# Block products by a seven-product scheme in the input products of a diffusion backbone's second block, and another order of the opening

## The reference, cut to what matters

```python
xx = h_shift - h
xr, xw, xk, xv, xa, xg = (h + xx * mu[m] for m in range(6))
r = xr @ w_r; k = xk @ w_k; v = xv @ w_v; zg = xg @ w_z     # 1024 x 2048 each
w_lo = tanh(xw @ w1); a_lo = xa @ a1                        # 1024 x (2*64) each
```

## Time and profile before

| | |
|---|---|
| median of 3 runs | 2981.92 us (2981.19 to 2993.5) |
| the profiled execution, own time | 2982.58 us |
| its span in the trace | 2980.7 us |
| mean granted TensorE clock | 0.954 |
| TensorE matmul | 2700.6 us busy, 91% |
| VectorE, ScalarE, GpSimd | 1448.8, 744.6, 266.5 us busy |

### The profile page before, as it was taken

The page is one execution under the profiler, slowest core; times in us unless marked ns, Lnnn a source line. Parts: engine busy times, 40 slices in busy tenths (PEclk is TensorE's granted clock), DMA queues, the critical chain, the costliest instruction groups (busy, mean ns, idle before and its releaser), DMA issues. The chain is left out here.

```text
span 2980.7 us, 73744 instructions
## 1 busy us (share of the span) xinstructions
PE 2700.6 (91%) x33498; PEld 1678.5 (56%) x33498; DVE 1448.8 (49%) x2198; ACT 744.6 (25%) x1311; POOL 266.5 (9%) x420
## 2 busy tenths in 40 slices
PE   5999999989999959999999998688898898888699
PEld 1555555543444534455555554477777777777543
DVE  3222222228999940230101000689989989888201
ACT  3121221212112100220100100445454454443100
POOL 1000000000000000000000000012212112121100
PEclk8999999999999979999999999699999999999699
DMA  4222222251313136333222231111111111110161
GB/s 183 72 90 87 83 90 83 83 175 35 106 45 97 36 123 227 126 98 103 91 93 92 95 101 66 36 30 39 40 36 41 38 35 45 40 29 28 54 238 50
DMA packets 211569, 242.83 MB, mean 81 GB/s; under 512 B 22952, under 2 KB 158456, under 8 KB 210133
## 3 DMA queue, kind: packets, MB, share of 16 engines
q1 hardware_dynamic: 199090, 194.97, 20.4%
q0 software_dynamic: 11552, 43.27, 3.9%
q10 hardware_dynamic: 644, 0.24, 0.0%
HBM read 184.95 MB, written 53.49 MB: 80 GB/s over the span
## 5 line engine op out<-in xcount | busy, mean ns | idle before, releaser
L105 PE MATMUL ps<-hT,hw 128*128 128x512 f32 (+1 forms) x2048 | 562.1, 435 | 5.5 <-ACT hT L119 5.5
L105 PEld LDWEIGHTS ps<-hT,hw 128*128 128x128 f32 x2048 | 313.0, 192 | 251.7 <-issue 251.7
L1751 POOL TENSOR_SCALAR e_Sd<-e_S,e_pcd 128x64 f32<-128x64 f32 x256 | 164.3, 658 | 779.3 <-DVE e_S L108 317.7
L105 PE MATMUL ps<-m_spare 128*128 128x512 f32 (+1 forms) x768 | 209.8, 434 | 0.0
L113 DVE TENSOR_SCALAR hcv<-hpad,hpc 128x641 f32<-128x641 f32 x48 | 29.6, 616 | 301.5 <-ACT hpad L119 301.5
L119 ACT ACT_TABLE_LOAD x87 | 111.6, 1283 | 239.6 <-PE ps L105 233.6
L105 PEld LDWEIGHTS ps<-m_spare 128*128 128x128 f32 x768 | 116.9, 191 | 91.8 <-issue 91.8
L119 ACT ACTIVATE m_w<-ps 128x640 f32<-128x640 f32 x64 | 45.1, 704 | 484.7 <-PE ps L105 484.7
L105 PE MATMUL ps<-f_w,f_y 128*128 128x512 f32 x320 | 140.2, 600 | 9.7 <-DMA f_y<-scratch_y_d 8.9
L116 DVE TENSOR_TENSOR m_w<-ps,m_w 128x640 f32<-128x640 f32 x16 | 13.2, 825 | 258.8 <-ACT m_w L119 258.8
L108 DVE SCALAR_TENSOR_TENSOR m_spare<-m_room,col 128x640 f32<-128x640 f32 (+2 forms) x32 | 21.0, 713 | 237.0 <-PE ps L105 237.0
(11 more groups left out here) (276 smaller groups left out, 4798.3 us busy)
## 6 DMA issues: line engine op xcount, KB each, us to landing
hw<-in_hy_w_in SPq DMA_DIRECT2D x64, 512.0 KB, 3.9
scratch_rkvz_d<-m_w POOLq DMA_DIRECT2D x64, 320.0 KB, 3.4
m_room<-in_ada_w SPq DMA_DIRECT2D x24, 512.0 KB, 6.5
scratch_vx_d<-hot POOLq DMA_DIRECT2D x32, 320.0 KB, 3.1
conv_room<-scratch_vx_d SPq DMA_DIRECT2D x8, 1280.0 KB, 9.1
aw<-in_ada_w SPq DMA_DIRECT2D x8, 1024.0 KB, 18.1
f_w<-in_rw_w_o SPq DMA_DIRECT2D x32, 256.0 KB, 4.1
scratch_g_d<-hg POOLq DMA_DIRECT2D x16, 320.0 KB, 2.5
```

What stands on the lines that cost most here:

```text
L105: return nc.tensor.matmul(out, lhsT, rhs, start=first, stop=last)
L1751: po_.did(nc.gpsimd.tensor_scalar(Sd[:, q, :], S_at[:, n, q, :], pcd[i % 3][:, u:u + 1], None, MUL), ("Sd", i, n))
```

## The change

Three things in `middle`, one in `startup`.

**Products.** The four first blocks of r are left as they are. The other 60 blocks are taken in 30 pairs `PAIRS` (6 of r, 8 each of k, v, z). A pair is a product of a 256 x 1024 by a 1024 x 640 matrix, cut into 2 x 2 blocks: output channels in two halves of 128, input channels in two halves of 512 (four groups, `KH`), tokens in two halves of 320 (`HT`). Seven block products (P1 to P7) take the place of eight, after the Winograd form of Strassen's scheme. Each is four `mm` of 128 x 320, into one bank of a ring of eight. Four sums of weight blocks `S` (128 x 512 each) are made on GpSimd per pair, and four sums of token blocks `T` (128 x 1280 each) on VectorE once per matrix. VectorE puts the results together by seven additions of 128 x 320 per pair; ScalarE copies P1. For z the sigmoid is taken of the finished result in SBUF, and VectorE multiplies in SBUF, in the next pair's turn.

**Weights.** SyncE fetches a pair at a time (1 MB) into one of three slots; two of them lie where the rows `x` and the bias were, so the first two loads wait until the last row tile is normalised.

**Order.** The small products w and a come right behind the first four blocks, and their mixes are made first. The mixes and token sums of the next matrix are spread over the pairs of the present one, two instructions in each (`beside`).

**The opening.** `ORDER` is another one, and the programs of VectorE and ScalarE follow it, as the diff shows.

```diff
-    ORDER = ["cond", "fcols", "F0", "bias", "a0", "cols", "a1", "x0", "x1", "F1", "x2", "a2", "x3", "x4", "a3", "x5", "x6", "a4", "x7", "F2",
-             "a5", "a6", "a7", "shift", "scale"]
+    ORDER = ["cond", "fcols", "bias", "a0", "F0", "x0", "a1", "x1", "a2", "F1", "x2", "a3", "x3", "cols", "a4", "x4", "F2", "a5", "x5", "a6",
+             "x6", "a7", "x7", "shift", "scale"]
+    COLS_AT = 4
...
+                channels(0)
                 sine(0)
-                channels(0)
-                channels(1)
+                for k in range(1, COLS_AT):
+                    channels(k)
                 sine(1)
-                for k in range(2, KD):
+                for k in range(COLS_AT, KD):
                     channels(k)
-                sine(2)
                 a.wait_ge(pe_.sem, pe_.now("a7"))
                 for c, at in enumerate(ROWS):
                     ac_.did(act(mrow[at, :], ps[at, 0:2, :].rearrange("p b n -> p (b n)"), ACT.Copy), ("half row", c))
+                sine(2)
...
+                        pe.wait_ge(ac_.sem, ac_.now(("h", COLS_AT - 1)))
...
+                    if k == COLS_AT:
+                        pe.wait_ge(dv_.sem, dv_.now("cols"))
...
-                argument(0)
-                v.wait_ge(pe_.sem, pe_.now("cols"))
-                dv_.did(nc.vector.tensor_copy(col[:, :, :], ps[:, 4, :].rearrange("p (g n) -> p g n", g=4)), "cols")
...
+                argument(0)
                 argument(1)
+                v.wait_ge(pe_.sem, pe_.now("cols"))
+                dv_.did(nc.vector.tensor_copy(col[:, :, :], ps[:, 4, :].rearrange("p (g n) -> p g n", g=4)), "cols")
...
+    PAIRS = [(b, q) for b in BIG for q in range(KE // 2) if (b, 2 * q) not in UNITS[0:U]]
+    HT = T // 2
+    KH = KD // 2
+    ORDER = ("P1", "P6", "P7", "P5", "P2", "P4", "P3")
+    TAKEN = {"P1": "p1", "P6": "U2", "P7": "U3", "P5": "U4", "P2": "C11", "P4": "C21", "P3": "C12"}
+    RESULTS = [(n, g) for g in range(len(PAIRS)) for n in ORDER]
+    bank = lambda n, g: ps[:, (4 + RESULTS.index((n, g))) % 8, 0:HT]
...
+        sums = [w2_at[:, U * T:U * T + KD * T], o_at[:, :]]
+        mix = [flat(a, KD) for a in mixes]
+        low = {"w": mix[1], "a": flat(sums[1], KD)}
+        TT = [[flat(a[:, n * KH * HT:(n + 1) * KH * HT], KH) for n in range(4)] for a in sums]
...
+        S = [flat(y_at[:, KD * T + 3 * D + n * KH * P:KD * T + 3 * D + (n + 1) * KH * P], KH) for n in range(4)]
+        rw2 = [flat(a, KD) for a in (spare[:, KD * T:KD * T + 2 * D], xb[:, 0:2 * D], xb[:, 2 * D:4 * D])]
...
+                def load_pair(g):
+                    b, q = PAIRS[g]
+                    slot = (g + 1) % SLOTS
+                    if g >= SLOTS:
+                        wait(pe_, "P3", g - SLOTS)
+                    sp.dma_start(rw2[slot], A[f"rw_w_{b}"][0].rearrange("(k p) n -> p k n", p=P)[:, :, 2 * q * P:(2 * q + 2) * P]).then_inc(s_rw2[slot], 16)
...
-                for m in range(U, len(UNITS)):
-                    load_unit(m)
+                wait(dv_, "normed", NT - 1)
+                load_pair(0)
+                load_pair(1)
+                wait(pe_, "proj", *UNITS[2])
+                for g in range(2, len(PAIRS)):
+                    load_pair(g)
...
+                def weight_sum(g, n):
+                    if g == len(PAIRS):
+                        return
+                    slot = (g + 1) % SLOTS
+                    A_ = lambda i, j: rw2[slot][:, j * KH:(j + 1) * KH, i * P:(i + 1) * P]
+                    po.wait_ge(s_rw2[slot], 16 * (g // SLOTS + 1))
+                    if g:
+                        wait(pe_, ("P5", "P6", "P7", "P3")[n], g - 1)
+                    if n in (1, 3):
+                        wait(po_, "S", g, n // 2)
+                    p, q, op = ((A_(1, 0), A_(1, 1), ADD), (S[0], A_(0, 0), SUB), (A_(0, 0), A_(1, 0), SUB), (A_(0, 1), S[1], SUB))[n]
+                    po_.did(nc.gpsimd.tensor_tensor(S[n], p, q, op), ("S", g, n))
+
+                def store(b, u):
+                    m = UNITS.index((b, u))
                     po.dma_start(A["rkvz_d"][BIG.index(b), u * P:(u + 1) * P, :], rout[m % U]).then_inc(s_o[m % U], 16)
+                for b, u in UNITS[0:U]:
+                    wait(ac_, "out", b, u)
+                    store(b, u)
+                wait(dv_, "normed", NT - 1)
+                for n in range(4):
+                    weight_sum(0, n)
+                for g, (b, q) in enumerate(PAIRS):
+                    for n in (2, 0, 1, 3):
+                        weight_sum(g + 1, n)
+                    if b == "z":
+                        wait(dv_, "gated_z", 2 * q + 1)
+                        store(b, 2 * q + 1)
+                        wait(dv_, "gated_z", 2 * q)
+                        store(b, 2 * q)
+                    else:
+                        wait(dv_, "C21", g)
+                        store(b, 2 * q + 1)
+                        wait(dv_, "C12", g)
+                        store(b, 2 * q)
...
-                for n in range(4, len(JOBS)):
-                    b, u = JOBS[n]
-                    steps, *label = TAKEN[n - 4]
-                    wait(steps, *label)
-                    weights(n)
+                        last = product(n, prompt, k)
+                    pe_.did(last, ("proj", *UNITS[n]))
+                pe.wait_ge(s_lw, 64)
+                for n, b in enumerate("wa"):
+                    wait(ac_, "out", *UNITS[n])
                     for k in range(KD):
-                        if u == 0:
-                            wait(dv_, "mix", b, k)
-                        product(n, image, 0, k)
-                        last = product(n, prompt, LS, k)
-                    pe_.did(last, ("proj", b, u))
+                        wait(dv_, "mix", b, k)
+                        lhsT = lw[n][:, k, :, :].rearrange("p z r -> p (z r)")
+                        mm(pair[n][:, image], lhsT, low[b][:, k, image], k == 0, k == KD - 1)
+                        last = mm(pair[n][:, prompt], lhsT, low[b][:, k, prompt], k == 0, k == KD - 1)
+                    pe_.did(last, ("lora", b))
+
+                for g, (b, q) in enumerate(PAIRS):
+                    slot = (g + 1) % SLOTS
+                    A_ = lambda i, j: rw2[slot][:, j * KH:(j + 1) * KH, i * P:(i + 1) * P]
+                    at = BIG.index(b) % 2
+                    B_ = lambda j, c: mix[at][:, j * KH:(j + 1) * KH, c * HT:(c + 1) * HT]
+                    T_ = TT[at]
+                    OPERANDS = {"P1": (A_(0, 0), B_(0, 0)), "P2": (A_(0, 1), B_(1, 0)), "P3": (S[3], B_(1, 1)), "P4": (A_(1, 1), T_[3]),
+                                "P5": (S[0], T_[0]), "P6": (S[1], T_[1]), "P7": (S[2], T_[2])}
+                    if g == 0:
+                        wait(ac_, "out", *UNITS[U - 1])
+                        wait(ac_, "lora", "a")
+                    pe.wait_ge(s_rw2[slot], 16 * (g // SLOTS + 1))
+                    if b != "r":
+                        wait(dv_, "mix", b, KD - 1)
+                    wait(dv_, "T", b, 3)
+                    for n in ORDER:
+                        at_ring = RESULTS.index((n, g))
+                        if at_ring >= 8:
+                            before, its = RESULTS[at_ring - 8]
+                            wait(ac_ if before == "P1" else dv_, TAKEN[before], its)
+                        if n in ("P5", "P6", "P7", "P3"):
+                            wait(po_, "S", g, ("P5", "P6", "P7", "P3").index(n))
+                        lhsT, rhs = OPERANDS[n]
+                        for k in range(KH):
+                            last = mm(bank(n, g), lhsT[:, k, :], rhs[:, k, :], k == 0, k == KH - 1)
+                        pe_.did(last, (n, g))
...
+                mixed("w", low["w"], range(KD))
+                mixed("a", low["a"], range(KD))
+                wait(dv_, "mix_prompt")
+                for n in range(4):
+                    token_sum("r", n)
...
+                    if share < 4:
+                        mixed(to, mix[at], (2 * share, 2 * share + 1))
+                    else:
+                        token_sum(to, 2 * share - 8)
+                        token_sum(to, 2 * share - 7)
...
+                for g, (b, q) in enumerate(PAIRS):
+                    m = UNITS.index((b, 2 * q))
+                    even, odd = rout[m % U], rout[(m + 1) % U]
+                    wait(ac_, "p1", g)
+                    wait(pe_, "P6", g)
+                    dv_.did(tt(u2, bank("P6", g), p1, ADD), ("U2", g))
+                    wait(pe_, "P7", g)
+                    wait(dv_, "U2", g)
+                    dv_.did(tt(u3, bank("P7", g), u2, ADD), ("U3", g))
+                    v.wait_ge(s_o[(m + 1) % U], 16 * (m // U))
                     v.wait_ge(s_o[m % U], 16 * (m // U))
-                    dv_.did(tt(rout[m % U], pair[n % 4][:, 0:T], sig, MUL), ("out", "z", u))
+                    wait(pe_, "P5", g)
+                    wait(dv_, "U3", g)
+                    dv_.did(tt(odd[:, HT:T], bank("P5", g), u3, ADD))
```

(91 more changed lines are left out.)

68 lines of the change are left out of this document (32 added, 36 removed).

## The result

The changed kernel takes 2910.57 us (median of 4 runs, 2907.56 to 2914.47), the kernel before beside it 2983.08 (4 runs, 2981.19 to 2993.5): ratio 0.9751, 95% interval 0.9725 to 0.9777. The forecast was 2908.6. One later execution of the changed kernel took 5009.94 us, at a mean granted clock of 0.833; it is left out of every median and interval. The profiled execution took 2912.12 us.

What follows compares the result with a forecast made beforehand. TensorE's own work was taken to bound the input products, gaps and low clock the opening. 67.5 - 1.1 - 5.8 - 0.55 + 14.0 = 74.0 us off 2982.6 gave 2908.6, own range 2901 to 2914, 8 in 10 2899 to 2924.

Steps and rivals of the forecast that it cites:

- Passes: TensorE's products: a 320-column pass costs 269 ns, a pair 15.07 us for 17.32, 67.5 us less over 30 pairs.
- Rival E: TensorE waits some 50 ns at semaphores for each of seven products: 10.5 us, 2919 in all; chance 0.07.
- Start of the pairs: Mixes and token sums hidden behind w and a; first P1 waits 1.1 us for ScalarE's copy of a's result.
- VectorE: VectorE's additions, mixes, token sums and multiplications in the pairs: at most 6.4 of 15.07 us, costing nothing.
- k's close place: Last pair of r: k's token sums end at 14.5 us, k's P1 due at 15.07; 0.6 us to spare.
- GpSimd: Pairs of r, k, v: sums of 1.26 us, 6.1 of 15.07 us with store issues; free up to 3.5 a sum.
- Rivals C and D: GpSimd's weight sums slower: C at 2.0 us each, 2922 in all, chance 0.13; D at 4.0 us, 3024, chance 0.04.
- z's loop: Sums queued behind z's late stores delay P6: 16.05 us a turn, not 15.07; 5.8 us over the last six pairs.
- End: After the last product, C12, sigmoid and multiplication precede the last store: 0.55 us more.
- Opening: New order in `startup`, bias and a0 in the idle 8.95 us: half rows at 49.2 for 63.16, 14.0 us less.
- Rival B: The opening stays at the low clock, as turned pieces and slices alternate: gain 0 there, 2922.6 in all; chance 0.14.
- The sum: Whole kernel: 67.5 - 1.1 - 5.8 - 0.55 + 14.0 = 74.0 us less than 2982.6.

Runs made afterwards that it cites:

- the first trace: Profiled execution of the changed kernel, without further edit, against the kernel before: 2912.12 us; median of its runs 2910.57 us, ratio 0.9751.
- the second: Trace of the changed kernel run again without edit, beside the kernel before: median 2908.97 us, ratio 0.9746.
- the third: Trace of the changed kernel run a third time without edit, beside the kernel before: median 2910.56 us, ratio 0.9754.

## Why the prediction was right

- *Passes: right.* The pair was to be 15.07 us and is 15.07 or 15.08. That the fixed part of a pass was taken as 3 ns, where the block before gave 4, had no reason in the text; it came out as 15.07 / 56 - 0.266 = 3 ns, which is luck, of 1.7 us at most. Rival E (50 ns at each product, 15.42 a pair) falls: the waits view has no such line.
- *Start of the pairs: right.* The wait for a's copy was 0.84 us (timeline at 1313.38), for 1.1. The token sums were done at 1309.3 and had 4.1 us to spare, for 5.7: they took 2.44 to 2.55 us each and not 1.49, since GpSimd's first sums ran beside them (below).
- *VectorE: right,* and k's close place was where the forecast put it: k's token sums end at 1403.18 and its first P1 starts at 1403.90, 0.7 us to spare for 0.6. It cost nothing as it stands, and 0.9 us with the sums doubled.
- *GpSimd: right.* A sum of 128 x 512 takes 1.26 us, as one of 2 x 512 did. Rivals C and D fall. (By D's own sum the whole would be slower than before from 3.6 us a sum, not 3.8, and it takes 2.0 us for the two stores of a pair where the chain had 2 x 0.54.)
- *z's loop: right in kind, too large in size.* The step "The loop from P6 to P6 is 16.05 us, not 15.07: 1.0 us for each of the last six pairs of z, 5.8 us" came to 15.77 and 4.1 us. From P6's start it gave 9.35 to the multiplications, 1.65 for them, 0.85 for the store, 3.9 for the sums, 0.3 to P6; the lines above give 9.29, 1.55, 0.84, 3.93 and 0.15. The latency and the multiplications, now from SBUF alone, were taken too long.
- *End: right.* P3's last pass ends at 1769.98 and the last store is issued at 1772.42, 2.44 us; before it was 1.89, from 1850.24 to 1852.13: the 0.55 of the forecast.
- Together 67.5 - 1.1 - 5.8 - 0.55 = 60.05 for the products, and 67.5 - 0.84 - 4.1 - 0.55 = 62.0 with the measured terms. The traces give 60.8 in the first and 60.8 to 61.9 over the four with this form of the products and no edit there.
- *Opening: right in kind, too small in size.* "Then I take the low clock as long as now, until 30.5" is the step that failed. The engine worked almost without a gap from 11.91, and the high clock came at 19.9 to 27, never at 30.5. The half rows began at 44.40 and 47.55 in the first two traces, for 49.2, and over the nine the gain was 15.5 to 18.9 us for 14.0. The upper bound of 18 us, by the high clock from 22 on, was just passed. Rival B (no high clock while turned pieces and slices take turns) falls: they do take turns at 0.77 and 1.90 us. Its reading that the rows "still" show 1.2 GHz at 41.43 was wrong: the clock had risen at about 31 us and fallen back, as the window view above shows. What the Trainium skill, page "TensorE: Matmul & The Clock Gate", section "Part 4: PE-mode transpose", says of transposes by themselves no run here shows: but for x3 and `cols` a slice or a filter layer always stood between two groups of them.
- *The sum* was 74.0, against 72.5 between the medians, and that it fits so well is luck in part: two errors cancel in it. The gain ahead of the scan was forecast too small (the opening's term by 1.5 to 4.9 us, the products' by about 1), and a loss behind it wasn't forecast. Of the gain at the scan's start 9.4 us are gone at the end of the first trace, 4.1 in the second (scan +2.2, rest +1.9), 2.3 in the third (scan 0.0, rest +2.3). The forecast had "What follows is the same": so it is as code, but not in time.

**What stays open.** The rest behind the scan took 183.1 to 185.4 us in all eleven traces with the new products and 179.6 and 181.3 in the two without. Its code is the same. Most of the difference lies ahead of the first product of `last_proj`, which follows the last `e_Sfin` by 27.4 to 30.2 us with the new products and by 25.2 and 26.5 without; what makes it is open, and two traces on one side are few.

## What to carry to other kernels

Where one engine is the bound and others stand idle, trading products for sums paid here what the passes' columns say, to 0.1 us a pair, as long as no store with a late wait stands in the queue ahead of sums that are due sooner. Here later stores, or the sums on VectorE, take the last 4 us from that part (2900.0 and 2904.84, 2907.47 and 2903.64 us in all, beside 2908.97 to 2910.57). Fill an opening's gaps with any product that is ready: it saves its own time, and here the high clock came by 27.1 us in all nine traces with the gap filled, for 28.7 in the one without.

## What was not expected of the hardware

**Two engines that exclude each other take turns, but not at once.** At the start of the pairs (timeline, VectorE and GpSimd, then TensorE):

```profile
1294.05 6.45 DVE L108 SCALAR_TENSOR_TENSOR m_o<-m_room,col 128x640 f32<-128x640 f32 x8
1296.88 6.15 POOL L1124 TENSOR_TENSOR m_y<-m_x 128x512 f32<-128x512 f32 x1
1300.42 1.48 DVE L116 TENSOR_TENSOR m_w<-m_spare 128x1280 f32<-128x1280 f32 x1
1301.94 2.44 DVE L116 TENSOR_TENSOR m_w<-m_spare,m_w 128x1280 f32<-128x1280 f32 x1
1303.18 2.32 POOL L1124 TENSOR_TENSOR m_y<-m_y,m_x 128x512 f32<-128x512 f32 x1
1304.30 2.55 DVE L116 TENSOR_TENSOR m_w<-m_spare 128x1280 f32<-128x1280 f32 x1
1305.46 2.51 POOL L1124 TENSOR_TENSOR m_y<-m_x 128x512 f32<-128x512 f32 x1
1306.77 2.55 DVE L116 TENSOR_TENSOR m_w<-m_spare,m_w 128x1280 f32<-128x1280 f32 x1
...
1313.38 2.39 PE L105 MATMUL ps<-m_spare,m_x 128*128 128x320 f32 x8 [0.84 <-ACT alo L119]
```

GpSimd's first sum waited through the last mixes and the first token sum and took 6.15 us for 1.26; from then on the two engines took turns, and each instruction of 1.49 or 1.26 us lasted 2.3 to 2.55. With the sums on VectorE nothing was stretched. The rule of the Trainium skill quoted ahead ("SBUF — State Buffer", "SBUF: two separate sides") gave 2.75 for both in a row. The trace agrees in kind: the token sums end at 1304.38, 1306.85 and 1309.32, so one of each takes 2.47 us, 0.28 less than in a row. Later in the pairs the two rarely meet, and in the changed kernel nothing of it reached TensorE.

**With gaps of 4.47 us the low clock came in mid-stage** (sums made twice), after 400 us at 1.00; with the gaps of 0.45 us in the changed kernel it did not. In the opening with `cols` early it came behind a gap of 3.37 us.

**The start of the high clock scatters** by 7 us over executions of one program (19.9 and 27.0), and so does the mean clock of the scan: 0.89 and 0.92 in two executions of the kernel with the sums on VectorE, 12.2 us apart.
